# A third Strassen step in the column groups of eight pairs, at later places, and plain column items at the end of w_ff2

## The reference, cut to what matters

```python
u = jnp.square(jax.nn.relu(jnp.einsum('bsd,df->bsf', h, w_ff1[l])))   # 2048 -> 8192
x = x + jnp.einsum('bsf,fd->bsd', u, w_ff2[l])                        # 8192 -> 2048
return rmsnorm(x, g_final)                                            # end of the first block
...
return (jax.nn.silu(gate) * val) @ w_down                             # second block, 5632 -> 2048
```

## Time and profile before

| | |
|---|---|
| median of 3 executions | 2425.72 us (2425.38 to 2426.73) |
| the profiled execution's own time | 2424.52 us |
| its span, first to last instruction | 2422.7 us (1.8 us lie around it) |
| busy: PE, PEld, DVE, ACT | 98%, 84%, 72%, 51% |
| mean granted clock of PE | 0.997 |
| first segment of `w_ff2` | 752.8 to 837.7 us of the span |
| last segment of `w_ff2` | 1275.8 to 1371.1 us |
| the groups of `w_down` | 1831.6 to 1908.7, 2087.1 to 2174.3, 2330.3 to 2422.7 us |

### The profile page before, as it was taken

One profiled execution on the slowest core, in us unless ns is written; L12 is line 12 of the kernel. 1 busy time (PEld: TensorE's weight loads), 2 busy tenths in 40 slices (PEclk: granted clock), 3 DMA queues, 4 the chain that ended last, 5 costly groups with the idle time before them and its releaser, 6 DMA issues.

```text
span 2422.7 us, 30747 instructions
## 1 busy us (share of the span) xinstructions
PE 2383.5 (98%) x12569; PEld 2035.3 (84%) x12569; DVE 1734.6 (72%) x1886; ACT 1225.2 (51%) x1437; POOL 0.2 (0%) x4
## 2 busy tenths in 40 slices
PE   9999999999999999999999899999998999999999
PEld 8788888888888888888887788888886888888877
DVE  6575656566578768778678767855778687887887
ACT  5454454455455444444445555555554455545553
POOL 0000000000000000000000000000000000000000
PEclk9999999999999999999999999999999999999999
DMA  7456566665555665655654555555564656565554
GB/s 249 157 184 195 167 190 189 194 192 189 191 176 204 224 199 191 200 182 182 216 184 171 168 165 166 174 182 183 182 192 156 192 176 191 197 201 184 183 181 165
DMA packets 238040, 452.15 MB, mean 187 GB/s; under 512 B 16569, under 2 KB 20779, under 8 KB 237771
## 3 DMA queue, kind: packets, MB, share of 16 engines
q1 hardware_dynamic: 237147, 449.07, 57.8%
q10 hardware_dynamic: 752, 1.12, 0.1%
HBM read 446.46 MB, written 3.67 MB: 186 GB/s over the span
## 4 chain that ended last, share of the span: by engine, by line
PE 91%; DVE 6%; ACT 1%; DMA 0%; issue 0%; DVEq 0%; ACTq 0%
PE PS L72 91%; DVE WL L72 2%; DVE TA L72 1%; DVE XT L72 1%; ACT WH L72 1%; DVE TB L72 0%; DVE PB L72 0%; DVE MHL L72 0%; DMA RAW<-in_w_down 0%; DVE PT L72 0%; ACT SQ L72 0%; ACT MHL L72 0%; DVE XHL L72 0%; ACT TA L72 0%; DMA VR<-in_g_mix 0%
## 5 line engine op out<-in xcount | busy, mean ns | idle before, releaser
L72 DVE TENSOR_TENSOR WL<-RAW,WH 128x1024 fp32r<-128x1024 f32 (+1 forms) x844 | 1003.1, 1202 | 491.5 <-ACT WH L72 488.7
L72 PE MATMUL PS<-XHL,WH 128*128 128x512 f32 x3984 | 1254.3, 396 | 5.7 <-DVE XHL L72 2.6
L72 ACT ACTIVATE WH<-RAW 128x1024 fp32r<-128x1024 f32 (+1 forms) x845 | 865.7, 1039 | 743.3 <-PE PS L72 717.6
L72 PEld LDWEIGHTS PS<-XHL,WL 128*128 128x128 f32 x3968 | 746.1, 188 | 176.3
L72 PE MATMUL PS<-XHL,WL 128*128 128x256 f32 x3968 | 780.5, 278 | 0.0
L72 PE MATMUL PS<-WH,MHL 128*128 128x512 f32 x1960 | 621.8, 392 | 20.6 <-DVE XT L72 12.5
L72 PEld LDWEIGHTS PS<-XHL,WH 128*128 128x128 f32 x3984 | 607.1, 188 | 10.3 <-DVE XHL L72 3.1
L72 PEld LDWEIGHTS PS<-WH,MHL 128*128 128x128 f32 x1960 | 369.2, 188 | 103.4 <-DVE XT L72 13.9
L72 PE MATMUL PS<-WL,MHL 128*128 128x512 f32 x980 | 382.5, 390 | 0.0
L72 PEld LDWEIGHTS PS<-WL,MHL 128*128 128x128 f32 x980 | 184.8, 189 | 36.9
L72 ACT ACTIVATE MHL<-TA 128x1024 fp32r<-128x1024 f32 x33 | 35.0, 1061 | 119.5 <-DVE TA L72 119.5
(11 more groups left out here) (150 smaller groups left out, 1279.8 us busy)
## 6 DMA issues: line engine op xcount, KB each, us to landing
RAW<-in_w_ff SPq DMA_DIRECT2D x256, 512.0 KB, 4.2
RAW<-in_w_in SPq DMA_DIRECT2D x224, 512.0 KB, 3.8
RAW<-in_w_up SPq DMA_DIRECT2D x176, 512.0 KB, 4.3
RAW<-in_w_down SPq DMA_DIRECT2D x88, 512.0 KB, 4.1
RAW<-in_w_mix_out SPq DMA_DIRECT2D x32, 512.0 KB, 4.0
RAW<-in_w_out SPq DMA_DIRECT2D x32, 512.0 KB, 3.7
RAW<-in_w_conv_out SPq DMA_DIRECT2D x16, 512.0 KB, 3.6
RAW<-in_w_attn_out SPq DMA_DIRECT2D x16, 512.0 KB, 4.1
```

Of the source, the lines that this page charges most:

```text
L72: ins = step[1](*step[2], **step[3])
```

## The change

Eight-pair groups get three Strassen steps, at the third, fifth and sixth pair (2, 4, 5 counted from 0), where they had two at the second and fourth; six-pair groups have theirs at the third and fourth pair in place of the second and fourth. The short block of a step comes second in place of last. `sums13` moves to one entry before `left`, `sums24` to right after the split of `left`. The buffers of the activations' sums grow to three, and `AS` shares the memory of `SQ`. In the last segment of `w_ff2` the second group becomes two plain items of 512 columns (`token_item`, L463), eight entries of twelve matmuls each and no Strassen step, with the transposes of quarters 0 and 1 in the first of them and of quarter 2 in the second. The item at L1337 is not changed, so it transposes quarter 2 once more.

```diff
-SEVEN = {8: (1, 3), 6: (1, 3)}
+SEVEN = {8: (2, 4, 5), 6: (2, 3)}
...
-            AXH = sb("AXH", [P, 2, 4, P], f32r, c=c)
-            AXL = sb("AXL", [P, 2, 4, P], f32r, c=c)
-            AS = sb("AS", [P, 4, P], c=c)
+            AXH = sb("AXH", [P, 3, 4, P], f32r, c=c)
+            AXL = sb("AXL", [P, 3, 4, P], f32r, c=c)
             EV = sb("EV", [P, 2, 512], c=c)
-            sb("QK2pad", [P, 4096 - 1536 - 2048], c=c)
...
+        AS = SQ[:].rearrange("p (a b) -> p a b", a=4)
...
-                        ents.extend((what, first) for what in ("left", "t13", "t24", "b22"))
+                        ents.extend((what, first) for what in ("left", "b22", "t13", "t24"))
...
-                for g in range(2):
+                for g in range(2 if seg < 3 else 1):
                     pairs(io["w_ff2"][0], 2048 * seg, k16, 1024 * g)
+            for g in (2, 3):
+                put(io["w_ff2"][0], k16, 512 * g, 2048 * 3)
...
             t_made[u] = V.step(tt, T24[:, 512:1024], RAW[:, a, 512:1024], T24[:, 0:512], sub)
+            return t_made[u]
...
+                if what == "left":
+                    t = sums24(u)
                 if done is not None:
                     raw_free[done] = t
                     load_to(done + NR)
                 state["split"] += 1
-                if i + 2 < len(ents) and ents[i + 2][0] == "left":
-                    sums13(ents[i + 2][1])
                 if i + 1 < len(ents) and ents[i + 1][0] == "left":
-                    sums24(ents[i + 1][1])
+                    u = ents[i + 1][1]
+                    load_to(u + 1)
+                    sums13(u)
...
                     for work in (((bp, a11, 0, o, c), (b, a12, 1, False, False)),
+                                 ((b + 2, s4, 0, False, False),),
                                  ((bp + 3, s1, 0, o, c), (bp + 2, s3, 1, o, c)),
-                                 ((bp + 1, s2, 0, o, c), (b + 1, a22, 1, False, False)),
-                                 ((b + 2, s4, 0, False, False),)):
+                                 ((bp + 1, s2, 0, o, c), (b + 1, a22, 1, False, False))):
...
+        def final_rest(gs, vs):
+
+            for g, v in zip(gs, vs):
+                x4 = XT[:, :, 512 * g:512 * g + 512]
+                a = squares(SUM1, g, 512, v)
+                yield
+                v = V.step(tt, x4, x4, GF[:, None, 512 * g:512 * g + 512].to_broadcast([P, 2, 512]), mul,
+                           after=[a, (s_gf, 16)])
+                tk["x", g] = v
+                yield
+                tk["sum"] = squares(SUM2, g, 512, v)
+                if g == 3:
+                    tk["both sums"] = tk["sum"]
+                yield
+
+        def final_group_evac(it):
+
+            s, b, ends = it
+            vs = []
+            for half in range(2):
+                x4 = XT[:, :, 512 * half:512 * half + 512]
+                vs.append(V.step(tt, x4, x4, PS[:, b + 2 * half:b + 2 * half + 2, :], add, after=ends[half]))
+                yield
+            free[s] = [vs[1]]
+            yield from final_rest((0, 1), vs)
+
         def final_evac(it, g):
-            s, b, ends = it
-            half = g % 2
...
+            s, b, t = it
             x4 = XT[:, :, 512 * g:512 * g + 512]
+            v = V.step(tt, x4, x4, PS[:, b:b + 2, :], add, after=[t])
+            free[s] = [v]
+            yield
+            yield from final_rest((g,), (v,))
...
-                mid = {6: [lambda: turn_x_item(0, G_AT2, nxt)], 7: [lambda: turn_x_item(1, G_AT2, nxt)]}
...
+                if seg == 3 and g:
+                    break
+                it = group_item(group(io["w_ff2"][0], 2048 * seg, ALLK, g), MHL, utok, stok)
+                later(final_group_evac(it) if seg == 3 else group_evac(it, g))
+        for g in (2, 3):
+            mid = ({4: [lambda: turn_x_item(0, G_AT2, nxt)], 6: [lambda: turn_x_item(1, G_AT2, nxt)]} if g == 2 else
+                   {5: [lambda: turn_x_item(2, G_AT2, nxt)]})
+            it = token_item(stream(io["w_ff2"][0], 2048 * 3, ALLK, 512 * g, 512, 2), MHL, utok, 512, mid)
+            later(final_evac(it, g))
```

More of the change, by code:

```diff
@@ L597, in sums_x @@
             v = V.step(tt, AS[:, 3, :], a12, AS[:, 1, :], sub)
-            a = A.step(act, AXH[:, seven], AS[:], AF.Copy, after=[v, ax_free.get(seven)])
-            tok[seven] = V.step(tt, AXL[:, seven], AS[:], AXH[:, seven].bitcast(f32), sub, after=[a])
+            a = A.step(act, AXH[:, seven], AS, AF.Copy, after=[v, ax_free.get(seven)])
+            tok[seven] = V.step(tt, AXL[:, seven], AS, AXH[:, seven].bitcast(f32), sub, after=[a])
         def group(w, row0, kcs, g):
@@ L1157, in ff_evac @@
             yield from sevens_x(g, 8, stok, [v])
+        def final_rest(gs, vs):
[20 more added lines that the diff above has]
+            yield from final_rest((0, 1), vs)
         def final_evac(it, g):
-            s, b, ends = it
-            half = g % 2
+            s, b, t = it
             x4 = XT[:, :, 512 * g:512 * g + 512]
-            v = V.step(tt, x4, x4, PS[:, b + 2 * half:b + 2 * half + 2, :], add, after=ends[half])
-            if half == 1:
-                free[s] = [v]
+            v = V.step(tt, x4, x4, PS[:, b:b + 2, :], add, after=[t])
+            free[s] = [v]
             yield
[L1168 to L1177, removed]
+            yield from final_rest((g,), (v,))
         nxt = {}
```

## The result

The changed kernel takes 2482.24 us (median of 4, 2481.28 to 2483.17); on the same chip the kernel before takes 2426.22 (2425.38 to 2427.84). The ratio is 1.023, with a 95% interval of 1.0212 to 1.0248: slower, as forecast, but by 56 us where 26 were worked out, and above the range. The profiled execution's span is 2479.7 us, against 2422.7.

The account below looks back on a forecast made before the run. PE was taken to bound the kernel, busy 98%, waiting nearly only for DVE. Terms -6.2 + 22.8 + 8.05 + 5.65 - 1.8 + 8.0 - 10.4 gave +26.1 us, a median of 2452, range 2432 to 2472.

Parts of the forecast that it names:

- matmuls: 27 fewer, 8 more transposes: Whole kernel: nine more steps save three matmuls each, 6.2 us less; eight more transposes at the block's end, 1.1 us.
- DVE in a group: Eight-pair groups: DVE's queue ends 32.7 us after the start against PE's 29.4; 3.3 us lost, 4.75 where a group follows.
- Six-pair groups, -1.8: w_down's six-pair groups: waits of 9.8 us become 8.05, as their steps adjoin too.
- `w_down`: Its eight-pair groups: middle segment +8.05 us, last segment +5.65; the waits at the starts of its groups stay.
- The clock, +8.0: Behind the five first eight-pair groups, waits of some 3.9 us cost 1.6 us each; nothing for waits of 2.4.
- Moved at no cost: the sums of activations: In w_ff1's items: the third step's sums, 9 more in all, cost nothing, since DVE has room there.
- w_ff2's 1.4 us of split waits: First three segments of w_ff2: today's waits for splits go, 1.4 us less.
- The end of the first block, -10.4: Plain items at w_ff2's end: waits and clock loss of 15.9 us become 5.5.
- The other estimate there, 0.5: Block's end: 0.5 us where the second plain item takes the banks of quarter 1's transposes.
- A: Rival: DVE's 97% still fits between PE's entries, nothing lost in groups of eight; 2403 us, chance 0.08.
- B: Rival: only groups' ends wait, at lower bounds 1.4 and 2.8 us, and the clock holds; 2424 us, chance 0.09.
- C: Rival: the next group's `sums13` waits for its transfer, 8.4 us at each of five first groups; 2470 us, chance 0.06.

Follow-up runs that it names:

- shorter sums: The changed kernel with each sum of weights made on 128 of 512 columns, all instructions and waits kept; 2428.33 us, ratio 1.0006 to the kernel before.
- filled kernel: The changed kernel with 148 matmuls by zeros ahead of the last entry of each group but the very last; 2466.24 us, ratio 1.0165.
- spread kernel: The changed kernel with a split put between the sums of activations for the fifth and sixth pair in each segment's last w_ff1 item; 2477.94 us.
- plain items alone: The kernel before with only the changed end of w_ff2 (two plain items, quarter 2 turned twice) and the changed buffers; 2416.74 us, ratio 0.996.
- two-step kernel: The changed kernel with two steps (pairs 2 and 4) in a group of eight in place of three; 2413.68 us, ratio 0.9944.

## Why the prediction was right in sign and wrong in size

The sum against what the two traces show, in us of the profiled span (PE's waits of more than 0.15 us behind 700 us of the span: 31.6 us in 17 before, 68.2 in 44 after):

| term | predicted | measured |
|---|---|---|
| matmuls: 27 fewer, 8 more transposes | -5.1 | the counts came |
| PE's waits | +26.4 (34.7 in groups, 12.7 gone and 4.4 new at the block's end) | +36.6 |
| clock, net | +4.8 (8.0, less 3.2 at the block's end) | +17.9 (22.79 less 4.84) |
| resuming behind a wait | not priced | +7.3 (27 more waits x 0.27) |
| sum | +26.1 | +57.0 (-5.1 + 36.6 + 17.9 + 7.3 = 56.7) |

The clock's row is half of every stretch at the 1.2 GHz level, less the part of it in which PE was idle. The sum missed 30.9 us: 13.1 in the clock, 10.2 in PE's waits (5 at the starts of `w_ff2`'s segments, 4 at the block's end, 1 in `w_down`), and 7.3 for resuming behind a wait, a term that it did not have. Which work sets the waits was right; what a wait costs beside its length was not.

**DVE in a group: held.** "Lost: 3.3 us a group", 4.75 where a group follows. In the first segment the first group has waits of 0.51, 0.39, 0.78 and 3.89 us, 5.6; the second 0.77 and 2.26, 3.0: 8.6 against 8.05. The sum itself can be laid beside DVE's and ACT's queues in the second group:

```profile
815.81 1.06 ACT L72 ACTIVATE WH<-RAW 128x1024 fp32r<-128x1024 f32 x1 [0.30 <-PE PS L72]
...
816.91 1.23 DVE L72 TENSOR_TENSOR WL<-RAW,WH 128x1024 fp32r<-128x1024 f32 x1
...
847.00 1.41 DVE L72 TENSOR_TENSOR XT<-XT,PS 128x512 f32<-128x512 f32 x2
```

From 816.91 to 848.41 are 31.5 us, where 31.4 were worked out. The 0.2 us up to ACT's copy, which no row stood for, are 0.1 (PE's `left` ends at 815.72). So following one engine's queue from its last wait, instruction by instruction, gave a wait right to a microsecond where the row did not exist before. The shorter sums showed that its terms are the cause for the larger part.

**Six-pair groups, -1.8: held.** All waits of that segment together went from 11.9 to 10.3 us. **`w_down`: held,** its waits in all three segments rose by 13.1 us against 11.9 forecast.

**The clock, +8.0: the step that failed most.** The traces show 22.8 us after and 4.8 before, a net of +17.9 where the sum had +4.8. The prediction took waits of 2.4 us for short enough, on the strength of one wait of 3.15 us that had kept 1.00. Five of the twelve slow stretches are the forecast ones; of the others four stand behind waits of 2.03 to 2.61 us, one at the third segment's start (below), one behind the transposes, and one, as before, in the groups of six. The five forecast ones cost 8.3 us, as priced; the other seven cost 14.5. The filled kernel showed the cost by itself: 16 us. The Trainium skill's page TensorE: Matmul & The Clock Gate, part 1, which makes the throttled state the default, was nearer to it than the row I chose. Five of the nine shorter waits kept the full clock, so the traces don't bear out that every one of them costs a stretch, either.

**Resuming: left out.** The bracket in the timeline counts from a modelled end. From 797.55 to 801.84 are 4.29 us; less the usual 0.228 us that is 4.06, not 3.89. And the first matmul behind a wait is followed after 0.34 us (784.04 to 784.38), not 0.228. That is 0.16 or 0.17, and 0.11 more, on nearly all of the 44 waits.

**"Moved at no cost: the sums of activations": wrong.** Two of them in a row held SP's loads back, as the spread kernel showed, for some 0.8 us of waits at a segment's start and 4.3 us of the time. The third segment had it worst:

```profile
1128.88 1.42 DVE L72 TENSOR_TENSOR PB<-RAW 128x512 f32<-128x512 f32 x2 [1.96 <-DMA RAW<-in_w_ff]
1130.41 2.29 DVE L72 TENSOR_TENSOR BIAS<-BIAS,CONST 128x2048 f32<-128x2048 f32 x1
```

There the late unit is followed in DVE's queue by the addition into `BIAS`, and PE waits 3.57 us in place of 1.01, with 6.8 us at half clock behind it. That `BIAS` makes the difference to the other segments is read from this order and not tested. DVE's weight sums have a share in the starts, too: with the shorter sums the waits there are gone in three segments and 2.3 us in the third. I had taken w_ff2's 1.4 us of split waits to go; waits at the starts of the segments came to 5.0 us in place of none.

**The end of the first block, -10.4: half right.** For the plain items alone it holds, 8.3 there and 10.5 in time. In the changed kernel only 3.4 us are won, since the group's steps cost 5.1 us of waits, 1.18 of it at the segment's start (3.3 forecast), and the needless turn 3.19 us and a slow stretch where the estimate was 0.6. The other estimate there, 0.5, came as 0.40.

**The rivals.** A, that 97% would still fit, fell: with two steps (73.9 of 84.4 us) PE is never idle, with three it waits. So did the reading that the engine of the highest occupancy is the one to relieve (the Trainium skill, Perfetto Trace Analysis, Identifying the Most-Contended Engine). Over the span it names PE (weight loads 84% before, 82% after) ahead of DVE, 72% before and after, while DVE set the end of the groups. B's lower bounds were passed at every end. C, a transfer that lands too late for `sums13`, did happen, but at the starts of segments, behind an item, and not between two groups, and by 1.2 to 2.2 us of DVE's time.

## What to carry to other kernels

Where an algorithm trades matmuls for vector work, count the vector engine's work in the stretch between its last forced wait and the next hand-over, not over the span: here the third step had 4.7 us more of DVE to pay for 0.7 us of PE. Then price a wait of PE for more than its length: here 0.27 us to resume, and the clock, which fell behind 12 of the 17 longest waits, at 1.9 us each on average (22.8 us in all). And when work moves to a "free" place, look at what the queue there was feeding, the loads above all.

## What the runs showed that was not expected

- The clock fell behind some waits of 2.0 to 2.6 us and not behind others of the same length, in the same execution (2.26 and 2.28 us above); nor does one place keep its outcome from kernel to kernel: behind 2.23 us at the start of `w_down`'s first group it fell in the two-step kernel and kept 1.00 in the changed one.
- Work that changes nothing can pay: 148 matmuls on zeros, 34 us of PE at 0.228, made the changed kernel 16 us faster.
- GpSimd takes 1.67 to 1.78 us for a sum of 128x512 float32, DVE 0.69.
